# Delta rule: 32x32 inverses on GpSimd through HBM instead of five doubling levels on TensorE, and the last w_down halves by token tile

## The chip, the cores and the metric

The kernel runs on one core of a Trainium2 chip. A NeuronCore has a matrix engine (TensorE, PE), three elementwise engines (VectorE, DVE; ScalarE, ACT; GpSimd, POOL), a queue for transfers (SyncE, SP) and 16 DMA engines between HBM and the on-chip memory (SBUF). Matrix results land in PSUM, eight banks of 128 x 512 f32, which GpSimd can't read. Each engine executes its own list of instructions in order; they wait for one another by semaphores. Transfers are issued by SP and by ScalarE, each with a queue of its own.

The metric is the device time of one execution in microseconds (us), median of several.

## The reference

Two transformer blocks over 256 tokens of width 2048, all in float32. The first has a chunked mLSTM, a gated delta rule with a short convolution ahead of it, and output projections under gates; the second has windowed attention, gated linear attention in both directions and a SwiGLU network of width 5632; each block ends in an RMS norm. The part that the change touches is the solve of the delta rule, for 16 heads of width 128:

```
a_mat = where(strict, beta * (k k^T) * decay, 0)
lhs   = a_mat + eye
sol   = triangular_solve(lhs, rhs, lower, unit_diagonal)
u     = w_val - w_k S ;  o = q S + (q k^T * decay) u
```

and the end of the second block:

```
x = x + (silu(h @ w_gate) * (h @ w_up)) @ w_down
return rmsnorm(x, final_norm_w)
```

## The kernel before

**Products.** Nearly all arithmetic is in products of 256 tokens (two token tiles of 128) with weights from HBM. A job is a block of 512 output columns (JOBS; dk0, mq0, ..., d3 for w_down). It is cut into halves of 256 contraction rows; there are NH = 780 halves. Each weight is split into a high part (ScalarE, weight_hi) and a low part (VectorE, weight_lo), so that a float32 product becomes three fast ones: for each half, 2 row blocks x 2 token tiles x 3 = 12 matmuls of 512 columns, lines 1289 to 1291.

**Slots.** Everything else is a side step. side_table() gives each a slot, which is the number of the half that it stands ahead of: TensorE executes in slot s the side steps of s and then product(s). ScalarE and VectorE execute their parts of the side steps of s and then the split of half s + 3 (AHEAD). The weight ring holds four halves (RING), the raw ring three chunks of 1 MB (RAW), each of two halves. SP issues the load of chunk ci once both halves of chunk ci - 3 are split, which is at the splits of slot 2 ci - 8. Rows of activations for w_out and w_down are split by split_rows in rings of three (LRING).

**Delta rule.** Four groups g of four heads; slots run from s = END[dz g] + 1 = 35, 107, 163, 235. dk, dss, dkscale, dkc prepare k; drhs, ddecay, dmask the decays; dsc (s + 8 to s + 13) the scores, whose units (8 blocks of 128 x 128 for each group: four heads, two token tiles) are in the blocks B0 and PB. Then the inverse of the unit triangular blocks is built by doubling: dlev0 (s + 14) starts with the identity less the first level, dT transposes it, and for levels 1 to 6 dX (line 989), dY for U (line 999) and dY for T (line 1004, not in the last level) multiply 128 x 128 by 128 x 64 f32 blocks, with a copy by ScalarE, a subtraction by VectorE, and masks (LVL) and memsets by GpSimd between them. dv, du0, dbu, du1, do use the inverse; donorm, dgate and dout (s + 38) finish.

**Memory.** block_table() and bank_table() list the lives of the blocks of 4 KB a partition in the arena, and of the four side banks of PSUM, in step order; settle() places them, and a user of a block or bank waits for the last reader of what was there.

**End.** After d3's last product, res4(3) adds both tiles to the residual, sqsum takes the squares, nscale (with GpSimd's power -1/2) the scale, final scales four blocks of 512 columns, and SP stores them as four transfers of 512 KB.

**Start.** cols0 transposes the first norm columns when they have landed; xturn("u1", m) transposes two blocks of x and writes their high and low parts, at slot m - 2.

Of the kernel before, what the change touches and what calls it, by code (L numbers as in the profile page):

```python
# [62 lines left out]
LEVELS = 7  # L63
# [4 lines left out]
def host_constants():  # L68
# [5 lines left out]
    levels = []  # L74
    for l in range(LEVELS):
        w = 2 << l
        levels.append((r // w == c // w) & (r % w < w // 2) & (c % w >= w // 2))
    first = base + levels + [np.where(c > r, NEG, 0.0)]
# [13 lines left out]
    return {"const_first": np.concatenate([np.asarray(m, f) for m in first], axis=1),  # L92
            "const_second": np.concatenate([np.asarray(m, f) for m in second], axis=1),
# [125 lines left out]
def side_table():  # L219
# [26 lines left out]
    for g in range(4):  # L246
# [13 lines left out]
        for q in range(6):  # L260
            put(s + 8 + q, "dsc", g, q)
# [5 lines left out]
        put(s + 30, "du0", g), put(s + 31, "dbu", g), put(s + 32, "du1", g)  # L267
        put(s + 33, "do", g, 0), put(s + 34, "do", g, 1)
        put(s + 35, "donorm", g), put(s + 36, "dgate", g)
        put(s + 38, "dout", g, 0), put(s + 38, "dout", g, 1)  # L270
# [79 lines left out]
    for n in range(4):  # L350
        s = END[f"d{n}"]
        put(s, "res4", n), put(s, "sqsum", "r4", n)
        if n < 3:
            put(s + 1, "fweight", n)
    put(NH, "nscale", "r4")
    for n in range(4):
        put(NH, "final", n)
# [3 lines left out]
def gla_at(put, hp, s, v, t):  # L361
# [4 lines left out]
    for hh in range(2):  # L366
        for z in range(3):
# [16 lines left out]
    "delta": ("dk", "dss", "dkscale", "dkc", "drhs", "ddecay", "dmask", "dsc", "dlev0", "dT", "dX", "dY", "dv", "du0",  # L384
# [6 lines left out]
    "ffn": ("res2", "fact", "fturn", "res4", "fweight", "final"),  # L391
# [5 lines left out]
    "pe": {"ddecay": ("rest", "a", "b", "c"), "dY": ("", "T"), "ggate1": ("", "r")},  # L397
    "act": {"gate1": ("tanh", "exp", ""), "ddecay": ("a", ""), "gsum": ("q", "k", "")},
    "dve": {"cols0": ("",), "nscale": ("mean", ""), "gate1": ("v", "z", "arg", "u", ""), "dss": ("", "ck"),
            "dY": ("T", "U"), "donorm": ("mean", ""), "mscore": ("w", "den"), "msq": ("mean", ""),  # L400
            "ggate1": ("v", ""), "gsum": ("end", "rest", ""), "gsq": ("mean", ""), "alog": ("b", "")},
    "pool": {"dlev0": ("first", "", "zero")},
}
for _engine, _names in {
# [3 lines left out]
               "ggate2 gkend gsq gout alog aturn aout fturn final",  # L408
        "dve": "cols xturn kept silu gate0 gate2 fsum rel0 rel1 convtap convsilu dkscale ddecay dsc dlev0 dv dbu do "
               "dgate mdec mm mden mgate mgated yb ya yres x1w ggate0 ggate2 gscore gstate ggated apv res2 res4 fact "  # L410
               "fturn fweight final",
        "pool": "nscale dss drhs dmask dX dY donorm dgate mrhs msq ya gsq"}.items():
# [4 lines left out]
def signals(engine, name, args, part):  # L417

    if name == "dX" and engine == "pool":
        return args[1] < LEVELS - 1  # L420
    if name == "dY" and engine == "pool":
        return args[1] + 2 < LEVELS
    if name == "dY" and part == "T":
        return args[1] < LEVELS - 1
# [4 lines left out]
    if name == "final" and engine == "act":  # L429
        return args[0] < 3  # L430
# [15 lines left out]
def block_table():  # L446
# [31 lines left out]
    for g in range(4):  # L478
# [8 lines left out]
        live(("U", g), ("dlev0", g), ("pe:du1", g))  # L487
# [45 lines left out]
def bank_table():  # L533
# [6 lines left out]
    for step in STEPS:  # L540
# [12 lines left out]
        elif name == "dY":  # L553
            t.append((step + ("U",), step, (("dve:dY:U",) + args,), None))
            if args[1] < LEVELS - 1:
                t.append((step + ("T",), step, (("dve:dY:T",) + args,), None))
# [61 lines left out]
def _build(nc, ctx, a, out):  # L618
# [238 lines left out]
    def tensor_program(e):  # L857
# [441 lines left out]
        for slot in range(-AHEAD, NH + 2):  # L1299
# [3 lines left out]
            if 0 <= slot < NH:  # L1303
                product(slot)
# [1055 lines left out]
```

## Time and profile before

| | |
|---|---|
| time, median of 3 runs | 2563.59 us (2562.94 to 2566.3) |
| profiled execution | 2556.28 us |
| its span | 2554.1 us |
| TensorE busy | 2512.2 us, 98% |
| VectorE / ScalarE / GpSimd busy | 57% / 47% / 8% |
| whole weight loads | 387 of 1 MB, 5.1 us each from issue to landing |

The profile page gives busy time by engine, the span in slices, the chain that ended last and groups of instructions. Matmuls are pipelined: two of them overlap in the records, so the spacing of their starts says what one costs, not its duration. An f32 matmul of the side steps is recorded as two instructions, a transpose as one. A wait shows as idle time before an instruction, with what released it.

### The profile page before, as it was taken

To read this page: it belongs to the slowest core of one execution; us is meant where nothing else is said; L and a number is where in the kernel's file an instruction comes from. 1 tells how busy PE (TensorE), PEld (TensorE's weight loads), DVE (VectorE), ACT (ScalarE), POOL (GpSimd) and SP (SyncE) were. 2 spreads that over 40 slices of the span, in tenths; PEclk is the share of its full clock that TensorE was granted. 3 is DMA by queue.
4 is the path that set the end of the run, shared out by engine and by line. 5 is a ranking of instruction groups with operands and counts; after the bars stand their busy time and mean duration, and the time that the engine had idled before them with its cause. 6 is when DMAs were issued, how large, how long until landed. Compare 5 with 4: busy or idle time off the path is not lost.

```text
span 2554.1 us, 29749 instructions
## 1 busy us (share of the span) xinstructions
PE 2512.2 (98%) x12194; PEld 2073.3 (81%) x12194; DVE 1455.3 (57%) x1732; ACT 1196.7 (47%) x1662; POOL 202.7 (8%) x147
## 2 busy tenths in 40 slices
PE   8999999999999999999989999999999999999998
PEld 7888888888888888888877778767788888888886
DVE  6654665475456644556664544546555555456675
ACT  6533453354245434555654444546444444445654
POOL 0032003202310130000000000000000000000000
PEclk9999999999999999999999999999999999999999
DMA  6543454254345434666546444335655655555553
GB/s 221 180 149 100 150 187 148 92 169 160 116 132 165 165 116 133 211 208 208 200 157 209 149 148 144 122 114 191 206 190 189 191 188 190 189 190 189 181 196 134
DMA packets 220968, 426.52 MB, mean 167 GB/s; under 512 B 13766, under 2 KB 16079, under 8 KB 220834
## 3 DMA queue, kind: packets, MB, share of 16 engines
q1 hardware_dynamic: 213248, 411.72, 49.0%
q10 hardware_dynamic: 7586, 12.92, 1.5%
q8 instruction: 96, 1.57, 0.2%
q14 instruction: 38, 0.31, 0.0%
HBM read 420.39 MB, written 4.23 MB: 166 GB/s over the span
## 4 chain that ended last, share of the span: by engine, by line
PE 67%; issue 29%; DVE 2%; DMA 1%; ACT 1%; POOL 0%; SPq 0%; ACTq 0%; POOLq 0%; DVEq 0%
PE gemm L1289 18%; PE gemm L1291 18%; PE gemm L1290 18%; PE side L862 3%; PE side L999 2%; PE side L989 2%; PE side L1004 1%; DMA arena<-x 1%; PE side L1211 1%; PE side L1246 1%; DVE arena L1686 1%; PE side L1225 1%; PE side L964 1%; DVE weight_lo L1680 0%; DMA arena<-in_x_dram 0%
## 5 line engine op out<-in xcount | busy, mean ns | idle before, releaser
L1680 DVE TENSOR_TENSOR weight_lo<-weight_raw,weight_hi 128x1024 fp32r<-128x1024 f32 x780 | 975.4, 1253 | 792.4 <-ACT weight_hi L1311 790.9
L1311 ACT ACTIVATE weight_hi<-weight_raw 128x1024 fp32r<-128x1024 f32 x780 | 821.3, 1055 | 785.9 <-PE gemm L1291 764.2
L1289 PE MATMUL gemm<-weight_hi,x_hi 128*128 128x512 f32 x2368 | 954.7, 403 | 0.0
L1291 PE MATMUL gemm<-weight_hi,x_lo 128*128 128x512 f32 x2368 | 927.0, 391 | 0.0
L1290 PE MATMUL gemm<-weight_lo,x_hi 128*128 128x512 f32 x2368 | 924.2, 390 | 0.0
L1289 PEld LDWEIGHTS gemm<-weight_hi,x_hi 128*128 128x128 f32 x2368 | 446.4, 189 | 96.4 <-issue 11.3
L1291 PEld LDWEIGHTS gemm<-weight_hi,x_lo 128*128 128x128 f32 x2368 | 445.5, 188 | 97.2
L1290 PEld LDWEIGHTS gemm<-weight_lo,x_hi 128*128 128x128 f32 x2368 | 446.8, 189 | 89.1 <-issue 2.4
L1289 PE MATMUL gemm<-weight_hi,lhs_hi 128*128 128x512 f32 x736 | 289.5, 393 | 5.7 <-DVE lhs_lo L1680 5.6
L1291 PE MATMUL gemm<-weight_hi,lhs_lo 128*128 128x512 f32 x736 | 287.2, 390 | 0.0
L1290 PE MATMUL gemm<-weight_lo,lhs_hi 128*128 128x512 f32 x736 | 287.0, 390 | 0.0
L1311 ACT ACTIVATE arena<-side 128x512 f32<-128x512 f32 x109 | 64.3, 598 | 277.7 <-PE side L989 151.5
L1289 PEld LDWEIGHTS gemm<-weight_hi,lhs_hi 128*128 128x128 f32 x736 | 138.6, 188 | 37.2 <-DVE weight_lo L1680 8.0
L2207 POOL TENSOR_TENSOR stats<-stats,minus_half 128x4 f32<-128x4 f32 (+3 forms) x19 | 27.7, 1457 | 1731.2 <-DVE stats L1683 1731.2
L1291 PEld LDWEIGHTS gemm<-weight_hi,lhs_lo 128*128 128x128 f32 x736 | 138.5, 188 | 29.3
L1290 PEld LDWEIGHTS gemm<-weight_lo,lhs_hi 128*128 128x128 f32 x736 | 138.7, 188 | 28.1
L1680 DVE TENSOR_TENSOR lhs_lo<-arena,lhs_hi 128x512 fp32r<-128x512 f32 x184 | 128.2, 697 | 0.5 <-ACT lhs_hi L1311 0.5
L862 PE MATMUL side<-constants,arena 128*128 128x128 f32 (+4 forms) x668 | 99.0, 276 | 23.6 <-DMA constants<-in_const_first_dram 7.4
L862 PEld LDWEIGHTS side<-constants,arena 128*128 128x128 f32 (+4 forms) x668 | 81.0, 141 | 44.2 <-issue 8.5
L1311 ACT ACTIVATE lhs_hi<-arena 128x512 fp32r<-128x512 f32 x184 | 113.3, 616 | 1.1 <-PE gemm L1291 1.1
L2207 POOL TENSOR_TENSOR arena<-arena,phase_constants 128x512 f32<-128x512 f32 x56 | 78.5, 1422 | 142.9 <-PE side L989 78.7
L1680 DVE TENSOR_TENSOR arena<-arena,side 128x512 f32<-128x512 f32 x48 | 31.2, 685 | 67.5 <-PE side L1004 57.9
(184 smaller groups left out, 1354.5 us busy)
## 6 DMA issues: line engine op xcount, KB each, us to landing
weight_raw<-in_w_in_dram SPq DMA_DIRECT2D x207, 1024.0 KB, 5.1
weight_raw<-in_w_out_dram SPq DMA_DIRECT2D x48, 1024.0 KB, 5.1
weight_raw<-in_w_gate_dram SPq DMA_DIRECT2D x44, 1024.0 KB, 5.2
weight_raw<-in_w_up_dram SPq DMA_DIRECT2D x44, 1024.0 KB, 5.2
weight_raw<-in_w_down_dram SPq DMA_DIRECT2D x44, 1024.0 KB, 5.1
arena<-rel_line ACTq DMA_DIRECT2D x8, 384.0 KB, 4.9
arena<-in_x_dram SPq DMA_DIRECT2D x4, 512.0 KB, 9.4
arena<-in_final_norm_w_dram ACTq DMA_DIRECT2D x4, 512.0 KB, 7.1
```

Source lines behind the costliest of these rows:

```text
L862: return e.transpose(o, i, IDN[0:n, 0:n])
L964: m = e.matmul(p[:, (h % 2) * T:(h % 2 + 1) * T], yk[:, h * T:h * T + P], y[:, h * T:(h + 1) * T], start=True, stop=True)
L989: m = e.matmul(packed(p, n, wd), BM[:, n], sided(Tt[:, n], wd, 0), start=True, stop=True)
L999: m = e.matmul(packed(p, n, wd), X[:, n], sided(U[:, n], wd, 1), start=True, stop=True)
L1004: m = e.matmul(packed(p, n, wd), U[:, n], sided(X[:, n], wd, 0), start=True, stop=True)
L1211: m = e.matmul(o, l, r, start=z == 0, stop=z == len(terms) - 1)
L1289: e.matmul(pair[i][:, :], xh[:, s], wh, start=first, stop=False)
L1290: e.matmul(pair[i][:, :], xh[:, s], wl, start=False, stop=False)
L1291: m = e.matmul(pair[i][:, :], xl[:, s], wh, start=False, stop=last)
L1311: return e.activation(o, i, ACT.Copy, scale=scale)
L1680: return e.tensor_tensor(o, x, y, op)
L2207: return e.tensor_tensor(o, x, y, op)
```

## The change

1. The levels of width 2 to 32 leave TensorE. nout(g) (SP's queue, s + 11) writes the 32 x 32 diagonal blocks of the units to HBM with eight transfers; nin(g) (ScalarE's queue, s + 13) reads them back so that a partition holds one whole block (32 blocks, each four times, for eight columns of the inverse each); dinv(g) (GpSimd, s + 13) solves them with 31 rounds of a multiply and a subtract; tout(g) (SP, s + 24) and tin(g) (ScalarE's queue, s + 26) bring the inverses back by way of HBM into the diagonal of Tt.
2. Levels 64 and 128 stay on TensorE: dT at s + 28, dX and dY at s + 29 to s + 32, on operands cut to the width. Units are read where they lie, without masks. The later steps stand four slots on (dv s + 33, dout s + 42). The order of the scores is 0, 1, 4, 2, 3, 5.
3. Start: seven matmuls on zeros ahead of cols0, xturn("u1", m) for m >= 2 one slot later.
4. End: for the last three halves (LRING), all products of token tile 0 stand ahead of those of tile 1, and a step tail(i) takes the place of res4(3), sqsum, nscale and final, tile by tile; eight stores of 256 KB.

```diff
-        put(s + 14, "dlev0", g)
-        put(s + 16, "dT", g, 0), put(s + 16, "dT", g, 1)
-        for l in range(1, LEVELS):
-            put(s + 15 + 2 * l, "dX", g, l), put(s + 16 + 2 * l, "dY", g, l)
-        put(s + 29, "dv", g, 0), put(s + 29, "dv", g, 1)
+        for z, q in enumerate((0, 1, 4, 2, 3, 5)):
+            put(s + 8 + z, "dsc", g, q)
+        put(s + 11, "nout", g), put(s + 13, "nin", g), put(s + 13, "dinv", g)
+        put(s + 24, "tout", g), put(s + 26, "tin", g)
+        put(s + 28, "dT", g, 0), put(s + 28, "dT", g, 1)
+        for z, wd in enumerate(LEVELS):
+            put(s + 29 + 2 * z, "dX", g, wd), put(s + 30 + 2 * z, "dY", g, wd)
+        put(s + 33, "dv", g, 0), put(s + 33, "dv", g, 1)
...
-        put(m - 2, "xturn", "u1", m)
+        put(m - 2 if m < 2 else m - 1, "xturn", "u1", m)
...
+        def nout(g):
+            e.dma_start(claim("S", g)[:, 0:SUB * SUB // 4], a["const_unit"][:, :]).then_inc(sem("dma:unit"), 16)
+            w.wait_ge(*at("dve:dsc", g, 4))
+            to = n_dram[g].rearrange("(i h b) r c -> i b r h c", i=2, h=HB)
+            B0, B1 = by_head(blk("B0", g)), heads(blk("PB", g), 0)
+            for b in range(NSUB):
+                s = slice(b * SUB, (b + 1) * SUB)
+                e.dma_start(to[0, b], B0[s, :, s]).then_inc(sem("dma:nout"), 16)
+                e.dma_start(to[1, b], B1[s, :, s]).then_inc(sem("dma:nout"), 16)
+        def tout(g):
+            w.wait_ge(*at("pool:dinv", g))
+            to = t_dram[g].rearrange("n (c q) r -> q n c r", q=4)
+            S = blk("S", g)[:, 2 * SUB * SUB // 4:3 * SUB * SUB // 4].rearrange("p (c r) -> p c r", r=SUB)
+            for q in range(4):
+                e.dma_start(to[q], S[q * SUB:(q + 1) * SUB]).then_inc(sem("dma:tout"), 16)
...
         for ci in range(CHUNKS):
+            while ci >= RAW and slot < 2 * (ci - RAW) - 1:
+                for name, *args in SIDE[slot]:
+                    if name in steps:
+                        steps[name](*args)
+                slot += 1
...
         def cols0():
+            w.wait_ge(sem("dve:zeros"), 1)
+            for i in range(7):
+                e.matmul(sides[3][:, :], xfer[:, 0:P], xfer[:, 0:NC], start=True, stop=True)
...
+        def dX(g, wd):
+            Tt, hw = units(blk("Tt", g)), wd // 2
+            if wd < P:
+                w.wait_ge(*at("act:dT", g, 1))
+                p = open_bank("dX", g, wd)
+                for n in range(2 * HB):
+                    for t in range(0, P, wd):
+                        s = slice(t, t + wd)
+                        m = e.matmul(p[s, n * hw:(n + 1) * hw], unit_of(g, n)[s, s], Tt[s, n, t:t + hw],
+                                     start=True, stop=True)
+            else:
+                w.wait_ge(*at("dve:dY", g, hw))
+                p = open_bank("dX", g, wd)
+                for n in range(2 * HB):
+                    m = e.matmul(p[hw:wd, n * hw:(n + 1) * hw], unit_of(g, n)[:, hw:wd], Tt[:, n, 0:hw],
+                                 start=True, stop=True)
             m.then_inc(sem("pe:dX"))
...
+            if slot == NH - LRING:
+                for idx in range(slot, NH):
+                    product(idx, (0,))
             if 0 <= slot < NH:
-                product(slot)
+                product(slot, (0, 1) if slot < NH - LRING else (1,))
...
+        def nin(g):
+            w.wait_ge(*at("dma:nout", g))
+            src = bass.AP(tensor=n_dram.tensor, offset=g * 2 * HB * NSUB * SUB * SUB,
+                          ap=[[0, 4], [SUB * SUB, P // 4], [1, SUB * SUB]])
+            e.dma_start(claim("N", g), src).then_inc(sem("dma:nin"), 16)
+        def tin(g):
+            w.wait_ge(*at("dma:tout", g))
+            w.wait_ge(*at("pool:dinv:zero", g))
+            src = t_dram[g].rearrange("(n b) c r -> b c n r", b=NSUB)
+            Tt = units(blk("Tt", g))
+            for b in range(NSUB):
+                s = slice(b * SUB, (b + 1) * SUB)
+                e.dma_start(Tt[s, :, s], src[b]).then_inc(sem("dma:tin"), 16)
...
+        def tail(i):
+            b, (r, hr), total = blk("x2", 3), scale_of("r4"), stat(NT, "total", "r4")
+            if i == 0:
+                w.wait_ge(*at("pe:xturn", "u3", 7))
+                w.wait_ge(*at("act:sqsum", "r2", 3))
+                w.wait_ge(sem("pe:first_tile"), 1)
+            else:
+                w.wait_ge(*out_of("d3"))
+            tt(part(b, i), part(b, i), pair_of("d3")[i][:, :], ALU.add).then_inc(sem("dve:tail"))
...
+        def dinv(g):
+            e.memset(claim("X", g), 0.0)
+            e.memset(claim("Tt", g), 0.0).then_inc(sem("pool:dinv:zero"))
+            N = blk("N", g).rearrange("p (r c) -> p r c", c=SUB)
+            U, tmp, V = (blk("S", g)[:, z * SUB * SUB // 4:(z + 1) * SUB * SUB // 4] for z in range(3))
+            U = U.rearrange("p (r c) -> p r c", r=SUB)
+            w.wait_ge(*at("dma:nin", g))
+            w.wait_ge(*at("dma:unit", g))
+            for j in range(SUB - 1, 0, -1):
+                n = SUB // 4 - j // 4
+                c = slice(j // 4, SUB // 4)
+                by = tmp[:, 0:j * n].rearrange("p (r c) -> p r c", c=n)
+                after(tt(by, over(N[:, 0:j, j], 2, n), over(U[:, j, c], 1, j), ALU.mult))
+                after(tt(U[:, 0:j, c], U[:, 0:j, c], by, ALU.subtract))
+            e.tensor_copy(V.rearrange("p (c r) -> p r c", r=SUB), U).then_inc(sem("pool:dinv"))
```

## Rows read from the trace of the kernel before

**Rows 1.** The page, busy time (share of the span) and instructions by engine.

```profile
PE 2512.2 (98%) x12194; PEld 2073.3 (81%) x12194; DVE 1455.3 (57%) x1732; ACT 1196.7 (47%) x1662; POOL 202.7 (8%) x147
```

**Rows 2.** Timeline, ScalarE's first and last of five splits: start, us, instruction [idle before].

```profile
1399.08 1.06 ACT L1311 ACTIVATE weight_hi<-weight_raw 128x1024 fp32r<-128x1024 f32 x1 [1.36 <-PE gemm L1291]
...
1409.96 1.06 ACT L1311 ACTIVATE weight_hi<-weight_raw 128x1024 fp32r<-128x1024 f32 x1 [1.72 <-PE gemm L1291]
```

**Rows 3.** The chain that ended last, group 0's first level: start us, us, what.

```profile
175.93 1.73 PE side L989 x16
180.48 1.73 PE side L999 x16
182.22 1.79 PE side L1004 x16
186.82 1.73 PE side L989 x16
```

**Rows 4.** Groups by line and form: busy us, mean ns | idle before.

```profile
L989 PE MATMUL side<-arena 128*128 128x64 f32 x384 | 45.4, 271 | 0.0
```

**Rows 5.** Timeline of TensorE, gscore and the step behind it.

```profile
1438.02 1.15 PE L1168 MATMUL side<-arena 128*64 128x64 f32 x32
1439.10 0.66 PE L862 MATMUL side<-constants,arena 128*128 128x128 f32 x4
```

**Rows 6.** Timeline, group 0's scores: slots 45 and 48 on TensorE, VectorE's part.

```profile
152.19 1.02 PE L964 MATMUL side<-arena 128*128 128x256 f32 x4
...
163.09 1.05 PE L968 MATMUL side<-arena 128*128 128x128 f32 x8
...
153.33 0.69 DVE L1680 TENSOR_TENSOR arena<-side,arena 128x512 f32<-128x512 f32 x1 [1.88 <-PE side L964]
```

**Rows 7.** The stores' line: issue time on SP, ns min/median/max.

```profile
L852 SPq DMA_DIRECT2D out_dram<-arena x4: 384/497/1232, 2546.8 to 2548.6; - x4
```

**Rows 8.** DMA issues: count, KB each, median us from issue to landing.

```profile
weight_raw<-in_w_in_dram SPq DMA_DIRECT2D x207, 1024.0 KB, 5.1
...
x<-arena ACTq DMA_DIRECT2D x4, 512.0 KB, 6.0
...
rel_line<-arena ACTq DMA_DIRECT2D x1, 32.0 KB, 3.7
```

**Rows 9.** Groups of GpSimd by form: busy us, mean ns | idle before.

```profile
L2207 POOL TENSOR_TENSOR arena<-constants,gate_work 128x512 f32<-128x512 f32 x16 | 16.3, 1040 | 42.4 <-PE side L862 42.4
L2207 POOL TENSOR_TENSOR arena<-arena,stats 128x1024 f32<-128x1024 f32 x8 | 16.1, 2011 | 1.1 <-DVE stats L1680 1.1
...
L2207 POOL TENSOR_TENSOR stats<-stats,minus_half 128x4 f32<-128x4 f32 x6 | 6.0, 1007 | 459.8 <-DVE stats L1683 459.8
...
L2207 POOL TENSOR_TENSOR stats<-stats,minus_half 128x2 f32<-128x2 f32 x5 | 3.5, 699 | 880.6 <-DVE stats L1683 880.6
```

**Rows 10.** Timeline of the end, after TensorE's last matmul.

```profile
2541.76 1.29 DVE L1680 TENSOR_TENSOR arena<-arena,gemm 128x512 f32<-128x512 f32 x2 [6.87 <-PE gemm L1291]
2543.08 0.60 ACT L1363 ACTIVATE side<-arena 128x512 f32<-128x512 f32 x1 [8.91 <-DVE arena L1680]
...
2544.78 0.17 DVE L1683 TENSOR_SCALAR stats<-stats 128x2 f32<-128x2 f32 x1
2545.03 0.70 POOL L2207 TENSOR_TENSOR stats<-stats,minus_half 128x2 f32<-128x2 f32 x1 [723.14 <-DVE stats L1683]
...
2545.97 1.95 ACT L1311 ACTIVATE arena<-arena,stats 128x512 f32<-128x512 f32 x3 [1.41 <-DVE stats L1683]
```

**Rows 11.** Timeline of VectorE: two splits, beside GpSimd's products and after them.

```profile
144.13 2.77 DVE L1680 TENSOR_TENSOR weight_lo<-weight_raw,weight_hi 128x1024 fp32r<-128x1024 f32 x1 [0.66 <-ACT weight_hi L1311]
...
148.44 1.22 DVE L1680 TENSOR_TENSOR weight_lo<-weight_raw,weight_hi 128x1024 fp32r<-128x1024 f32 x1
```

**Rows 12.** Timeline of TensorE, matmuls of the first product.

```profile
12.51 0.63 PE L1289 MATMUL gemm<-weight_hi,x_hi 128*128 128x512 f32 x1
12.94 0.63 PE L1290 MATMUL gemm<-weight_lo,x_hi 128*128 128x512 f32 x1
```

More of the change, by code:

```diff
@@ L73, in host_constants @@
     base = [(r == c), (r > c), (r <= c), np.ones((P, P))]
[L74 to L78, printed above, removed]
+    first = base + [np.where(c > r, NEG, 0.0)]
+    column = (P // SUB) * np.arange(SUB // 4)[None, None, :] + (np.arange(P) // SUB)[:, None, None]
+    unit = np.arange(SUB)[None, :, None] == column
     same = r // GL_C == c // GL_C
@@ L349, in side_table @@
         put(s, "fact", n), put(s + 1, "fturn", n, 0), put(s + 2, "fturn", n, 2)
-    for n in range(4):
+    for n in range(3):
         s = END[f"d{n}"]
[L352 to L357, printed above, removed]
+        put(s, "res4", n), put(s + 1, "sqsum", "r4", n), put(s + 3, "fweight", n)
+    for i in range(NT):
+        put(NH, "tail", i)
     return side
@@ L670, in at @@
         if signal.startswith("dma:"):
-            return sem(signal), DMAS[signal]
+            return sem(signal), DMAS[signal] * (args[0] + 1 if args else 1)
         return sem(signal), ORDINAL[(signal,) + args]
-    DMAS = {"dma:rel0": 32, "dma:rel1": 16, "dma:ggate1": 64, "dma:const2": 16}
+    DMAS = {"dma:rel0": 32, "dma:rel1": 16, "dma:ggate1": 64, "dma:const2": 16,
+            "dma:nout": 128, "dma:nin": 16, "dma:unit": 16, "dma:tout": 64, "dma:tin": 64}
     def blk(*name):
@@ L982, in dX @@
-        def dX(g, l):
-            wd = 2 << l
-            BM, Tt = units(blk("BM", g)), units(blk("Tt", g))
-            w.wait_ge(*(at("pool:dlev0", g) if l == 1 else at("pool:dX", g, l - 1)))
-            w.wait_ge(*(at("act:dT", g, 1) if l == 1 else at("dve:dY:T", g, l - 1)))
-            p = open_bank("dX", g, l)
-            for n in range(2 * HB):
-                m = e.matmul(packed(p, n, wd), BM[:, n], sided(Tt[:, n], wd, 0), start=True, stop=True)
-            m.then_inc(sem("pe:dX"))
@@ L1259, in fturn, with product @@
             turn_pair(p, blk("z", f"fg{n}"), c).then_inc(sem("pe:fturn"))
-        def product(idx):
+        def product(idx, tiles=tuple(range(NT))):
             j, c, h = HALVES[idx]
@@ L1286, in product @@
                     continue
-                for i in range(NT):
+                for i in tiles:
                     s = slice(i * P, (i + 1) * P)
@@ L2300, in ya, with tail @@
             tt(b, b, blk("z", f"ga{n}"), ALU.add).then_inc(sem("pool:ya"))
+        def tail(i):
+            w.wait_ge(*at("dve:tail:mean", i))
+            power(scale_of("r4")[0][:, i:i + 1], stat(NT, "total", "r4")[:, i:i + 1]).then_inc(sem("pool:tail"))
         def gsq(hp):
@@ L2304, in gsq @@
             power(stat(2 * NT, "grr", hp), stat(2 * NT, "gssq", hp)).then_inc(sem("pool:gsq"))
[L2306 to L2307 removed]
+        steps = dict(nscale=nscale, dss=dss, drhs=drhs, dmask=dmask, dinv=dinv, donorm=donorm,
+                     dgate=dgate, mrhs=mrhs, msq=msq, ya=ya, gsq=gsq, tail=tail)
         for name, *args in STEPS:
```

254 lines of the change are left out of this document (122 added, 132 removed).

## The prediction, made before the change was run

> **What bounds the kernel now.** I read the page's busy shares first: TensorE's matmuls are busy 98% of the span, no other compute engine over 57% [rows 1]. The slots prove that this is a real bound and not only a long queue: where TensorE has nothing but weight products, one half of a chunk (12 matmuls) takes (1409.96 - 1399.08) / 4 = 2.72 us, slot after slot [rows 2]. ScalarE starts one weight split in each of them, and its start is set by the product that frees a ring place. So the end is the sum of TensorE's products and of the side steps put between them, and the question for each edit is how much of TensorE's own stream it takes away, and whether TensorE then waits for something that it did not wait for before. The chain of waits in order of time gives the side steps of the delta rule: 16 instructions each (8 matmuls in two passes) of the lines of dX, dY for U and dY for T [rows 3].
>
> **The inverses on TensorE.** From one dX to the next dX is 186.82 - 175.93 = 10.89 us [rows 3]. Two products are 2 x 2.72 = 5.44, so one level costs 5.45. Six levels less the T half of the last (1.79) [rows 3] are 6 x 5.45 - 1.79 = 30.9 us for a group of four heads, and four groups 124 us, all on the path. The count agrees: 384 dX instructions are 4 groups x 6 levels x 16 [rows 4].
>
> What stays: dT (eight transposes) is moved, not changed. New per group are dX for 64 with 16 matmuls (32 instructions), dY for 64 with 32 (64), dX for 128 and dY for 128 with 8 each (16 and 16): 128 instructions for 272. They are smaller: stationary operands of 64 or 32 columns, and for width 64 two tiles in turn at partitions 0 and 64. The nearest row is gscore, 128x64 stationary with its outputs in turn in the two halves of the partitions: 32 instructions between 1438.02 and 1439.10, 0.034 us each [rows 5]; the old form takes 1.73 / 16 = 0.108 [rows 3]. I take 0.034 for the 96 of width 64 (3.3 us) and, for the 32 of width 128, which stay in one half, the middle, 0.057 (1.8 us), and 0.1 for each of four changes from product to side step (a level shows 5.45 for 5.25 of side steps in two of them): 5.5 us. Saving 30.9 - 5.5 = 25.4 a group, **101.6 us** in all. Bounds: all at 0.108 leaves 30.9 - 14.2 = 16.7 (67 us in all); all at 0.034 gives 26.2 (105 us).
>
> The Trainium skill, "TensorE: Matmul & The Clock Gate", section on what happens when you issue a matmul, says that a weight load takes its number of columns over 1.2 GHz, so 107 ns for 128 columns and 53 for 64. The 0.108 of the old form agrees; gscore's 0.034 is below 53, so there loads of the two halves overlap. By the page alone the 128 new instructions would cost at most about 6.8 us where I take 5.1: 7 us more in all.
>
> **The new way round: where a wait may come back.** Take group 0 (s = 35); in the three others s, too, is odd, and between s+14 and s+28 there are only evictions and, in groups 1 and 3, one mnum, so the pattern repeats. Slots 43 to 48 carry the scores: slot 45's start at 152.19 and slot 48's at 163.09, 3.63 apart [rows 6]. Score 4 now comes at slot 45; VectorE's step there ends at 153.33 + 0.69 = 154.0 [rows 6]. dT is at slot 63: slot 49 starts at 166.7, and 14 bare slots of 2.72 later is 204.8. Between the two, **50.8 us**, lie in a row:
> - nout: eight DMAs on SP's queue. An issue takes about 0.5 us there (384/497/1232 ns) [rows 7], and the smallest stores to and from HBM land after 3.7 us [rows 8]: 4.0 + 3.7, lands at 161.7. ScalarE, whose nin is at slot 48, reaches it near 161 and waits little.
> - nin: 512 KB on ScalarE's queue, 6.0 us like the x stores [rows 8]: 167.7.
> - dinv on GpSimd: 31 rounds of a multiply and a subtract, each waiting for the one before. The elements are j x (8 - j // 4) summed over j = 31 to 1, 1560, twice 3120. From 128x512 (1040 ns) and 128x1024 (2011 ns) an element costs 1.90 ns and an instruction 0.07 us; from the powers of 2 and 4 columns (699 and 1007 ns) the fixed part is 0.39 us [rows 9]. A hand-over adds 0.08 (2544.78 + 0.17 to 2545.03) [rows 10]. So 62 x (0.15 to 0.47) + 5.9 + 0.5 for the copy = 16 to 36 us; I take 26, the middle, as neither row has short three-dimensional operands.
> - tout: four DMAs on SP, 2.0 + 3.7 = 5.7. SP reaches it only after the weight load at slot 58, near 194.
> - tin: four DMAs on ScalarE's queue, 5.7; ScalarE reaches its slot 61 near 198.
>
> 167.7 + 26 = 193.7, tout lands at 199.7, tin at 205.4: **0.6 us after TensorE comes for dT**. tout further stands behind a 1 MB weight load (5.1 us to land [rows 8]) issued just before it on the same queue, which can add up to about 3 us. I take 1.5 us of stall a group, 6 in all; bounds 0 and 12 us a group.
>
> The skill speaks against this edit: "DMA: Bandwidth & Descriptors", Specifications, wants at least 512 B a run and says that shorter ones are read, modified and written. nout, tout and tin move runs of 128 B. No row of before has a thousand such runs in one transfer. By it the three transfers would be nearer the long end, which is the rival "late" below.
>
> What waits behind the waits: behind nout and tout SP holds the weight loads. The load next after tout is due near 199 and is needed by ScalarE at slot 65, about 210; a load takes 5.1 us, so some 6 us of delay are covered. Behind nin and tin ScalarE holds its weight splits, which run three slots (8.2 us) ahead of their products: covered up to about 5 us. Behind tin's semaphore TensorE holds everything; that is the stall counted. GpSimd has no other step between s+13 and s+25 in any group; its next, msq at s+26 in two of them, comes after. VectorE is slowed while GpSimd multiplies: one weight_lo took 2.77 us at 144.13, and 1.22 at 148.44, when GpSimd was through [rows 11]. In these slots VectorE has one split (at worst 2.8 us in a slot of 2.72) and little else, and runs three slots ahead: nothing added. The level masks, memsets and the packed subtractions that go were hidden behind products: 0. The steps four slots on end in dout(3) at slot 277; the products that read it begin at slot 290: 0. The load of the phase constants, 64 KB instead of 512, comes after the start and beside products: 0.
>
> **Start.** The first products run with 0.43 us between matmuls (12.51 to 12.94) [rows 12] where 2.72 / 12 = 0.227 is usual; the clock view grants 1.00 there all the same, but the spacing is that of the lower level, 1.2 GHz. About eight matmuls do: 1.6 us. The seven zero matmuls (14 instructions of 512 columns, 0.43 each at 2.4 GHz and twice that at 1.2) fill TensorE from about 1.4 us to 9 to 13 us, while the first transposes could start at 7.4. So the clock's 1.6 us is won or as much lost; xturn one slot later lets the first product go before x's second part lands, about 0.3. Sum: **-0.5**, from -1.5 to +2.5.
>
> **Tail.** The last product ends just before VectorE's residual at 2541.76 [rows 10], near 2541.65; the span is 2554.1, so 12.4 us follow. Now the first token tile's tail lies under 18 matmuls (4.1 us) of the second. After the last: residual 0.65 (half of 1.29), square and its read 0.9, mean and power 0.35 + 0.8, two copies of 0.65 [rows 10], four issues on SP of 0.5 and a landing of the last near 3.5 instead of 2 MB of stores at once: 0.1 + 0.65 + 0.9 + 1.15 + 1.4 + 1.5 + 3.5 = 9.2. Gain **3.1**, from 2 to 4. The order of the three last halves adds no matmul, and their splits are ready: the last pair of rows needs the product before them, 2.7 us ahead of its use.
>
> **Sum.** Against the profiled execution, 2556.28 (span 2554.1): -101.6 + 6 - 0.5 - 3.1 = -99.2, 2457.1. The runs' median, 2563.59, is 7.3 above that execution, and I carry this over: **2464.4**.
>
> **Rivals.** *Late:* TensorE waits at dT(g, 0) because dinv is at its long end (36 us) or the 128 B runs land late. Each us past the 50.8 us costs four. With 5 to 12 us a group: 2479 to 2506, middle about 2488. For: the chain fits with no margin, and nothing in before measures its small pieces. Against: mine are not the cheapest values. *No shorter matmuls:* small tiles cost 0.108 each, as if the weight load of a full tile set the pace: 8.7 us more a group, 2499. Gscore's row speaks against. *Slower than before:* GpSimd's small instructions cost like the powers of 2 to 4 columns in full, 0.7 to 1.0 us, plus 0.08. It decides from dinv = 26 + 25 = 51 us on, 0.73 us an instruction and hand-over; at 0.93 us dinv is 58, the stall 33 a group, 132 in all, SP holds the weight loads meanwhile, and the time is about 2563.6 - 105 + 132 = 2590. Its power function speaks against, since the time grows with 154 ns an element, so that it is no price of a product. *Without effect:* stalls and savings cancel, 2563.
>
> **How the numbers follow.** Forecast 0.58 (2450 to 2478: all matmuls at 0.034 and no stall to 3 us of stall more a group); late 0.28; no shorter matmuls 0.07; slower 0.05; without effect 0.02. The range 2450 to 2495 holds the forecast and some two thirds of late. What a measurement of this kernel can tell from no change is about 0.2%, 5 us: faster 0.93, same 0.02, slower 0.05.
>
> **What would show it.** Right: TensorE's idle before dT's transposes at most 3 us; the side steps between slots 63 and 67 of a group sum to some 5.5 us; GpSimd's 62 instructions span 26 us; no wait of ScalarE's weight_hi on a weight load in these stretches; the end 9 us after the last matmul. Wrong: dT waits for the DMA of Tt, with its place in GpSimd (dinv ends after 194) or in the queues (dinv ends before, tin lands after 205); small matmuls spaced by 0.1 us; or a product waiting on weight_lo after tout.

## The result, and the profile after

The changed kernel takes **2508.87 us** (median of four runs, 2505.57 to 2511.7) against 2563.27 for the kernel before, run beside it: ratio 0.9783, 95% interval 0.977 to 0.9795. It is 2.2% faster, but 44.5 us slower than forecast and 14 us above the range. The profiled execution took 2509.5, its span 2507.8. The case that came true is the rival *late*: TensorE waits for dT in every group. With what hangs on the wait it costs 10.8 us a group, inside the 5 to 12 of that rival; the time is 3 us beyond its 2506 because other terms fell short too.

The page of the profiled execution after: busy time by engine, then the chain that ended last by engine (beside [rows 1]).

```profile
PE 2435.0 (97%) x11632; PEld 1983.1 (79%) x11632; DVE 1418.9 (57%) x1705; ACT 1191.0 (47%) x1647; POOL 229.2 (9%) x328
...
PE 85%; POOL 5%; DMA 3%; DVE 2%; issue 1%; ACT 1%; ACTq 0%; SPq 0%; POOLq 0%; DVEq 0%
```

TensorE's busy time fell by 77.2 us, the span by only 46.3. GpSimd, idle 91% of the time, now holds 5% of the chain: an engine that does little is on the path. The view of waits shows where (TensorE's waits: us in total, times, longest):

```profile
PE side L889 <- DMA arena<-delta_inverses: 32.8, 4, 8.9
PE side L889 <- DVE arena L1755: 13.0, 8, 3.6
```

L889 is the transpose helper, here in dT; it waits 8.2 us a group on average for the inverses from HBM. The chain of waits from the scores of group 0 to that dT (start us, us, what; only the pieces used below):

```profile
161.06 11.21 DMA arena<-delta_blocks
172.67 1.33 POOL arena L2281
...
186.00 1.22 POOL arena L2281
187.29 0.32 POOL arena L2281
...
204.85 0.67 POOL arena L2337
205.54 0.67 SPq L852
...
207.55 1.97 DMA delta_inverses<-arena
209.54 0.33 ACTq L1532
...
210.90 3.71 DMA arena<-delta_inverses
214.66 1.97 PE side L889 x8
```

And what TensorE does around it, in the timeline (start us, us, instruction [idle before]) and, below, in windows of 5 us (busy us and count by engine, then PEclk, DMA share, GB/s):

```profile
205.84 0.39 PE L1335 MATMUL gemm<-weight_hi,x_lo 128*128 128x512 f32 x1
214.66 1.97 PE L889 MATMUL side<-constants,arena 128*128 128x128 f32 x8 [8.43 <-DMA arena<-delta_inverses]
...
218.55 0.63 PE L1335 MATMUL gemm<-weight_hi,x_lo 128*128 128x512 f32 x1
218.98 0.63 PE L1333 MATMUL gemm<-weight_hi,x_hi 128*128 128x512 f32 x1
```

```profile
205.00:210.00 5.00, 1.22 (x6) 0.68 (x4) 0.00 (x0) 0.00 (x0) 0.52 (x1) 1.00 0.27 39
210.00:215.00 5.00, 0.34 (x2) 0.35 (x3) 2.36 (x2) 2.00 (x2) 0.00 (x0) 0.51 0.71 224
215.00:220.00 5.00, 5.00 (x17) 4.23 (x16) 1.23 (x1) 2.14 (x3) 0.00 (x0) 0.50 0.64 210
220.00:225.00 5.00, 5.00 (x52) 4.04 (x51) 0.52 (x1) 1.93 (x3) 0.00 (x0) 0.97 0.01 3
```

In the wait the granted clock drops to 0.50, the 1.2 GHz level, and stays there until about 220: dT takes 1.97 us where the same kind of eight takes 1.03 at 2.4 GHz, and some nine matmuls are 0.43 apart, not 0.23. That is 0.9 + 9 x 0.2 = 2.7 us more, so this wait of 8.4 us costs 11. The groups differ: behind the 8.9 us of group 2 only three matmuls are slow, behind the waits of groups 1 and 3 ten and eleven. In all, TensorE's busy time is 10.4 us above that of experiment 4, which has the same instructions and no wait at dT (2435.0 and 2424.6): 2.6 us a group on average.

### The profile page after: what moved, and what is told of

It is laid out like the page before. It is cut to its first block, busy times and chain, and to the rows that moved or that the text cites. A ratio compares the mean times of both kernels' runs of the same rounds, so it can differ in the third digit from the quotient of the medians.

```text
span 2507.8 us, 28796 instructions
## 1 busy us (share of the span) xinstructions
PE 2435.0 (97%) x11632; PEld 1983.1 (79%) x11632; DVE 1418.9 (57%) x1705; ACT 1191.0 (47%) x1647; POOL 229.2 (9%) x328
## 4 chain that ended last, share of the span: by engine, by line
PE 85%; POOL 5%; DMA 3%; DVE 2%; issue 1%; ACT 1%; ACTq 0%; SPq 0%; POOLq 0%; DVEq 0%
PE gemm L1333 25%; PE gemm L1335 25%; PE gemm L1334 25%; POOL arena L2281 5%; PE side L889 3%; DMA arena<-delta_blocks 2%; DMA arena<-x 1%; PE side L1254 1%; DVE arena L1755 1%; DVE weight_lo L1749 1%; PE side L1289 1%; PE side L1268 1%; PE side L994 0%; ACT weight_hi L1361 0%; PE side L899 0%
## 5 line engine op out<-in xcount | busy, mean ns | idle before, releaser
L1749 DVE TENSOR_TENSOR weight_lo<-weight_raw,weight_hi 128x1024 fp32r<-128x1024 f32 x780 | 960.0, 1233 | 799.2 <-ACT weight_hi L1361 797.7
L2281 POOL TENSOR_TENSOR stats<-stats,minus_half 128x4 f32<-128x4 f32 (+4 forms) x20 | 28.2, 1408 | 1757.6 <-DVE stats L1752 1757.6
L2281 POOL TENSOR_TENSOR arena<-arena 128x48 f32<-128x48 f32 (+21 forms) x256 | 133.0, 520 | 381.5 <-DVE arena L1755 300.6
L889 PE MATMUL side<-constants,arena 128*128 128x128 f32 (+4 forms) x668 | 104.7, 286 | 56.0 <-DMA arena<-delta_inverses 32.8
L889 PEld LDWEIGHTS side<-constants,arena 128*128 128x128 f32 (+4 forms) x668 | 83.0, 146 | 80.6 <-DMA arena<-delta_inverses 34.5
L1361 ACT ACTIVATE arena<-side 128x512 f32<-128x512 f32 (+2 forms) x93 | 54.6, 588 | 167.4 <-PE side L889 92.8
L1430 ACT ACTIVATE arena<-gemm,stats 128x512 f32<-128x512 f32 x66 | 41.8, 685 | 46.6 <-PE gemm L1335 46.6
```

Source lines behind the costliest of these rows:

```text
L889: return e.transpose(o, i, IDN[0:n, 0:n])
L1361: return e.activation(o, i, ACT.Copy, scale=scale)
L1430: s = e.activation(part(b, i), pair_of(key)[i][:, :], ACT.Tanh, scale=hr[:, i:i + 1])
L1749: return e.tensor_tensor(o, x, y, op)
L2281: return e.tensor_tensor(o, x, y, op)
```

## The experiments

Each ratio is to the kernel before, run again beside the experiment; its interval is 0.3 to 0.5% wide, 8 to 12 us. The first four go at the cause from four sides: the number of the rounds, their length, their layout, and the time allowed.

**1. Only one round of elimination.**

```diff
-            for j in range(SUB - 1, 0, -1):
+            for j in range(1, 0, -1):
```

> The changed kernel with 1 of the 31 rounds of elimination on GpSimd left in each group (two instructions instead of 62, so the inverses are wrong); all transfers stay. Theory A, the chain through GpSimd (its 33 us of rounds) is simply too long for the four slots: the wait for dT falls from 8.0 to 9.3 us a group to nothing, the half clock after it goes too (2.6 us a group), and the time is 2461 to 2467. Theory B, the transfers are what is late (short runs of 128 bytes behind the weights on the queues): the wait falls by less than half, 2485 to 2500. Theory C, the loss is not in the wait but in GpSimd working beside VectorE: below 2460, and clearly below what moving the readers later (run e4_later4) gives.

Measured: 2466.19 us, ratio 0.9627 [0.9607, 0.9647]. 1.0 us of the wait for the inverses is left in all. Theory A: the transfers alone, 128-byte runs and all, would have been in time.

**2. Ten products more a group.**

```diff
                 after(tt(U[:, 0:j, c], U[:, 0:j, c], by, ALU.subtract))
+                if j % 3 == 0:
+                    after(tt(by, over(N[:, 0:j, j], 2, n), over(U[:, j, c], 1, j), ALU.mult))
```

> The changed kernel with ten of the products on GpSimd done twice in each group (72 instructions instead of 62, nothing else changed): by the durations of these shapes in the profile (0.24 to 0.48 us, with 0.08 between two) that is 4.6 us a group. Theory A: each us lands in the wait for dT in full, +18 to +20 us, 2527 to 2529; theory B: part of it hides beside the transfers, under +10.

Measured: 2524.16 us, ratio 0.9854 [0.9831, 0.9877]: 15 us over the changed kernel by the medians, 18 by the ratios. The forecast of the experiment, +18 to +20, is missed by a little: the 72 instructions span 36.22, 37.60, 36.22 and 37.23 us, 3.6 to 4.1 more than the 62 and not 4.6, 15.4 in all. Of these 13.6 are in the wait for dT, which rose from 32.8 to 46.4 us. So what the rounds take longer, TensorE waits longer, nearly in full.

**3. U kept by columns**, fewer and longer rows in each instruction (the constant, tout's source and the copy change with it).

```diff
-                by = tmp[:, 0:j * n].rearrange("p (r c) -> p r c", c=n)
-                after(tt(by, over(N[:, 0:j, j], 2, n), over(U[:, j, c], 1, j), ALU.mult))
-                after(tt(U[:, 0:j, c], U[:, 0:j, c], by, ALU.subtract))
+                by = tmp[:, 0:j * n].rearrange("p (c r) -> p c r", c=n)
+                after(tt(by, over(N[:, 0:j, j], 1, n), over(U[:, c, j], 2, j), ALU.mult))
+                m = tt(U[:, c, 0:j], U[:, c, 0:j], by, ALU.subtract)
...
```

> The same inverses with U kept by columns on GpSimd, so that the patterns of an instruction have 1 to 8 rows of up to 31 elements instead of up to 31 rows of 1 to 8 elements, and the copy at the end goes (0.66 us). If an instruction's price follows its rows (0.19 us, 8.7 ns a row and 0.85 ns an element, fitted to the shapes of the changed kernel's trace) the 62 take 26 us instead of 32.5, the wait falls to about 2 us a group, and the time by 27 to 37 us: 2472 to 2482. If it follows elements, only the copy is saved: -3, 2506.

Measured: 2512.98 us, ratio 0.9809 [0.9794, 0.9824]. Both expectations missed. The 62 instructions took 33.12 us where they had taken 32.45; the price by rows, which I had fitted to the mean durations of the shapes, doesn't show. Those means mixed two kinds of the same shape. Taken one by one, GpSimd's and VectorE's instructions read like this in the changed kernel (timeline, one stretch of group 0):

```profile
180.03 0.27 POOL L2281 TENSOR_TENSOR arena<-arena 128x48 f32<-128x48 f32 x1
180.37 1.21 POOL L2281 TENSOR_TENSOR arena<-arena 128x48 f32<-128x48 f32 x1
181.66 0.30 POOL L2281 TENSOR_TENSOR arena<-arena 128x69 f32<-128x69 f32 x1
...
180.21 1.23 DVE L1749 TENSOR_TENSOR weight_lo<-weight_raw,weight_hi 128x1024 fp32r<-128x1024 f32 x1 [1.50 <-ACT weight_hi L1361]
```

The first two have one shape; one takes 0.27 us, the other, which began while VectorE's weight_lo ran, 1.21, and ends 0.14 after weight_lo does (180.21 + 1.23 = 181.44). In group 0, 11 of the 62 are like this and take 13.1 us together; the other 51 take 14.5, 0.28 each. With U by columns other instructions meet the split (the two of 31 elements take 0.26 and 0.25, the first of 30 takes 1.23), again 11 of them, and the sum stays. Experiment 5 tests whether the split is the cause.

**4. Four slots more for the chain.**

```diff
-        put(s + 24, "tout", g), put(s + 26, "tin", g)
-        put(s + 28, "dT", g, 0), put(s + 28, "dT", g, 1)
+        put(s + 26, "tout", g), put(s + 28, "tin", g)
+        put(s + 32, "dT", g, 0), put(s + 32, "dT", g, 1)
...
```

(and each step from dX to dout four slots later).

> The changed kernel with the inverses as they are, their readers (dT and all steps behind it) another four slots later and the transfers out and in two slots later: TensorE has 17 us more work before it comes for dT. Theory A: the wait of 8 to 9 us and the half clock behind it go: 2461 to 2468. Theory B (what is late is the queue of transfers, which starts later too): some 5 us a group stay, 2480 to 2490. Theory C (GpSimd's work beside the others costs): over e1_norounds by 5 us or more. Rival of its own: steps four slots later collide with those of the mLSTM and the next group, 2475 to 2490 with waits on VectorE.

Measured: 2466.01 us, ratio 0.9629 [0.9614, 0.9645], the time of experiment 1, with the inverses made in full. Theory A; C falls, since GpSimd's rounds beside the others cost nothing that these runs can tell. (The 17 us in the expectation are wrong: the steps behind dT move with it, and four bare slots are 4 x 2.72 = 10.9 us. That still covers 8 to 9.) The transfers moved too, and not all is hidden: in group 0 a product waits 2.33 us, because ScalarE's splits stand behind tin, which waits for the inverses to reach HBM.

```profile
218.12 0.50 PE L1333 MATMUL gemm<-weight_hi,x_hi 128*128 128x512 f32 x1 [2.33 <-DVE weight_lo L1749]
```

**5. VectorE's splits cut to an eighth beside the inverses**, so that the low parts of the weights there are stale.

```diff
+            first = (idx % 2) * n
+            if any(END[f"dz{g}"] + 1 + 16 <= idx <= END[f"dz{g}"] + 1 + 34 for g in range(4)):
+                n = n // 8
-            tt(wlo[:, idx % RING, 0:n], raw[:, idx // 2 % RAW, (idx % 2) * n:(idx % 2 + 1) * n],
+            tt(wlo[:, idx % RING, 0:n], raw[:, idx // 2 % RAW, first:first + n],
```

> The changed kernel, with VectorE's subtraction that makes weight_lo done on one eighth of its elements (128 of 1024 columns) in 19 halves of each group, from 12 slots before dT to seven behind it; the rest of those low parts is stale, so the products there are off. In the trace of the changed kernel 12 of GpSimd's 62 instructions take 1.1 to 1.3 us instead of 0.3, and each ends when a weight_lo that began beside it ends. Theory D, the two engines shut each other out while both read two operands of SBUF: the long ones vanish, the 62 take about 62 x (0.29 + 0.08) = 23 us instead of 33, no wait for dT is left: 2463 to 2468. Rival: the length comes from a transfer or from GpSimd itself, 33 us and 2509 stay.

Measured: 2468.37 us, ratio 0.9621 [0.9602, 0.9641]. The inverses of group 0 in the timeline of this kernel, and in that of the changed one:

```profile
172.38 22.94 POOL L2284 TENSOR_TENSOR arena<-arena 128x31 f32<-128x31 f32 x62 [21.89 <-DMA arena<-delta_blocks]
```

```profile
172.34 32.45 POOL L2281 TENSOR_TENSOR arena<-arena 128x31 f32<-128x31 f32 x62 [21.50 <-DMA arena<-delta_blocks]
```

Nothing of GpSimd's work was changed, and it fell by 9.5 us; no instruction is over 1 us any more. So theory D: a GpSimd instruction that starts while VectorE subtracts two SBUF operands isn't through until that has ended.

The trace of the changed kernel has the contrast that the run lacks. Of the 248 instructions of the four groups 46 are long, and each ends 0.11 to 0.21 us after a VectorE instruction that began before it and reads two operands in SBUF: 44 times weight_lo, twice another. The six VectorE instructions there with an operand in PSUM (gemm) lengthen none. Group 1, VectorE and then GpSimd:

```profile
447.28 1.28 DVE L1755 SCALAR_TENSOR_TENSOR arena<-arena,gemm 128x512 f32<-128x512 f32 x2
...
449.75 1.32 DVE L1755 SCALAR_TENSOR_TENSOR arena<-arena 128x1024 f32<-128x1024 f32 x1
```

```profile
448.02 0.32 POOL L2281 TENSOR_TENSOR arena<-arena 128x66 f32<-128x66 f32 x1
...
450.06 1.16 POOL L2281 TENSOR_TENSOR arena<-arena 128x60 f32<-128x60 f32 x1
```

The Trainium skill, "SBUF — State Buffer", section "Who interferes with whom", says just this: a VectorE instruction with two SBUF inputs and a GpSimd instruction that reads SBUF hold a read port in turn, whole instructions long, whichever starts first. Both directions are in this case: [rows 11] show the other, 2.77 us for a weight_lo beside GpSimd.

**6. dT one slot later, transfers in place.**

```diff
-        put(s + 28, "dT", g, 0), put(s + 28, "dT", g, 1)
+        put(s + 29, "dT", g, 0), put(s + 29, "dT", g, 1)
...
```

> The changed kernel with dT and all steps behind it one slot later, transfers where they are. One bare slot is 2.72 us of TensorE's work, so the wait falls from 8.5 to 5.8 us a group. If TensorE's clock still falls to 1.2 GHz in the shorter wait: -11 us, 2498. If it doesn't: -21 us, 2488.

Measured: 2509.02 us, ratio 0.9784 [0.9765, 0.9803]; nothing was gained. In groups 0 and 2 the wait for dT fell as expected, to 6.1 and 6.3 us. In groups 1 and 3 it went over to another step. Timelines of group 1: TensorE at mout, ScalarE, and GpSimd's msq.

```profile
468.69 1.11 PE L889 MATMUL side<-constants,arena 128*128 128x128 f32 x4 [9.74 <-DVE arena L1755]
...
460.45 1.82 ACTq L1532 DMA_DIRECT2D arena<-delta_inverses  x4
462.31 0.47 ACT L1576 ACTIVATE arena<-side,stats 128x256 f32<-128x256 f32 x1 [13.06 <-issue]
...
464.53 1.01 POOL L2281 TENSOR_TENSOR stats<-stats,minus_half 128x4 f32<-128x4 f32 x1 [8.00 <-DVE stats L1752]
```

msq's squares (L1576) are at the slot of tin, s+26, and stand behind tin on ScalarE, which waits for the inverses to reach HBM. mgated needs msq, and mout, at s+28, needs mgated. So an mLSTM step waits for the delta rule through ScalarE's queue.

**7. nin as four DMAs.**

```diff
-                          ap=[[0, 4], [SUB * SUB, P // 4], [1, SUB * SUB]])
-            e.dma_start(claim("N", g), src).then_inc(sem("dma:nin"), 16)
+                          ap=[[SUB * SUB, P // 4], [1, SUB * SUB]])
+            for q in range(4):
+                e.dma_start(N[q * SUB:(q + 1) * SUB], src).then_inc(sem("dma:nin"), 16)
...
```

> The changed kernel with nin (512 KB into 128 partitions, one DMA whose outermost dimension has four entries) as four DMAs of 32 partitions each. The single one took 11.2 us from its issue, and in most of it the DMA engines were busy to 0.26, as if 4 of 16 worked. Theory E: the split brings it over all 16, it lands 4 to 6 us earlier, less three more issues of 0.5 us on ScalarE's queue; the wait for dT falls by 3 to 5 us a group: 2489 to 2497, lower if the half clock behind the wait shrinks too. Rival: the weight load issued 0.9 us earlier holds it up; it lands when it did, 2509.

Measured: 2494.88 us, ratio 0.9726 [0.9704, 0.9747]. In the chain of waits of this kernel, from nin's last issue to the first round:

```profile
161.78 0.47 ACTq L1525
162.28 5.38 DMA arena<-delta_blocks
168.06 0.28 POOL arena L2283
```

5.4 us from the last issue and 6.8 from the first, instead of 11.2, and GpSimd starts at 167.72 instead of 172.34. The wait for dT is 19.6 us in all, for 32.8. In the packets of the two traces nin moves from 164.4 to 171.3 in the changed kernel and from 164.0 to 167.0 here. So the bytes, their runs and the weight load before them are the same, and the rival of the experiment is out; what changed is the outermost dimension, 32 for 4, and the number of DMAs. One DMA with its dimensions in another order was not run. The changed kernel between the weight loads (windows of 1 us, DMA share next to last):

```profile
166.00:167.00 1.00, 1.00 (x6) 0.84 (x5) 1.00 (x2) 0.00 (x0) 0.00 (x0) 1.00 0.25 98
167.00:168.00 1.00, 1.00 (x7) 0.81 (x6) 0.27 (x1) 0.00 (x0) 0.00 (x0) 1.00 0.26 106
```

The Trainium skill, "DMA: Bandwidth & Descriptors", "Rules for kernel authors", has the rule: a DMA whose outermost dimension is a broadcast of c copies runs on at most c of the 16 engines. The share of 0.25 to 0.26 in the changed kernel agrees with 4 of 16.

**8. Experiment 4 with the old start.**

```diff
-        put(m - 2 if m < 2 else m - 1, "xturn", "u1", m)
+        put(m - 2, "xturn", "u1", m)
...
-            for i in range(7):
-                e.matmul(sides[3][:, :], xfer[:, 0:P], xfer[:, 0:NC], start=True, stop=True)
...
```

> The kernel of e4_later4 (readers of the inverses four more slots on) with the start of the kernel before: no seven matmuls on zeros, xturn in its old slots. The changed kernel's slot 43 began 1.27 us later than before's, although its first products run at the full clock. If that is the price of the new start: 1.3 us under e4_later4, 2464.7. If the forecast's sum held (-0.5 for the new start) and the 1.27 us come from elsewhere: 0.5 over it. The difference is near what the runs can tell; the trace at slot 43 decides.

Measured: 2463.53 us, ratio 0.961 [0.9587, 0.9633]. The intervals of 4 and 8 overlap, so the runs don't settle it; the traces do. Slot 43's scores begin at 145.00 here, at 146.20 in experiment 4 and in the changed kernel, at 144.93 before: the new start costs 1.2 us. Of the versions run, this has the lowest time.

**9. Experiment 4 with tout and tin in their old slots.**

```diff
-        put(s + 26, "tout", g), put(s + 28, "tin", g)
+        put(s + 24, "tout", g), put(s + 26, "tin", g)
```

> The kernel of e4_later4 with the transfers out and in back in their old slots (tout two slots earlier, tin two slots earlier), dT and the rest four slots later as there. In e6_later1 the wait left dT in the second group and came up whole (9.74 us) at mout, one step ahead: its msq stands on ScalarE's queue behind tin's wait for the inverses. Theory F, tin's place decides as much as dT's: in the second and fourth group TensorE waits 9 to 11 us at mout, with some half clock behind it: 2486 to 2494. Rival: only dT's distance counts: 2466.

Measured: 2496.67 us, ratio 0.9737 [0.9721, 0.9754]: 28 us over experiment 4 by the ratios, 31 by the medians, for two transfers *issued from earlier slots*. TensorE's timeline in groups 0 and 1:

```profile
214.00 0.80 PE L1333 MATMUL gemm<-weight_hi,x_hi 128*128 128x512 f32 x1 [4.88 <-DVE weight_lo L1749]
```

```profile
465.51 1.12 PE L889 MATMUL side<-constants,arena 128*128 128x128 f32 x4 [11.27 <-DVE arena L1755]
```

Theory F, with more than it said: mout waits 11.3 us in group 1, and in group 0 a *product* waits, since ScalarE's weight splits stood behind tin too ([12.73 <-issue] before the first of three) and used up their lead. The time is 3 us above the experiment's range, which counted no wait in groups 0 and 2.

**10. Two slots later, transfers with them.**

```diff
-        put(s + 28, "dT", g, 0), put(s + 28, "dT", g, 1)
+        put(s + 30, "dT", g, 0), put(s + 30, "dT", g, 1)
...
```

> The changed kernel with readers and transfers two slots later instead of four: 5.4 us more for the chain. Theory A and F: no wait at mout, since tin now comes after msq; 8.0 to 9.3 less 5.4 leaves 3 us at dT, 12 us in all, and 0 to 10 us of half clock behind it: 2478 to 2488. If a wait of 3 us leaves the clock at 2.4 GHz, the low end.

Measured: 2477.97 us, ratio 0.9664 [0.9648, 0.9681], at the low end of what was expected, though the clock did fall. The waits of TensorE for the inverses are two, together 8.9 us, in groups 0 and 2:

```profile
PE side L889 <- DMA arena<-delta_inverses: 8.9, 2, 5.0
```

In group 0, where TensorE waits 5.03 us, the granted clock averages 0.83 between 215 and 225, and the twelve transposes from dT on take 2.5 us until the next product starts, for 1.2 in experiment 4. In group 1 dT doesn't wait at all, and mout 1.55 us.

## Why the prediction was wrong, step by step

**What held.** The bound (TensorE's own stream) and the price of the small matmuls. Without the wait the kernel comes to 2463.5 to 2468.4 (experiments 1, 4, 5, 8). The forecast of 2464.4 has 6 us of stall in it; without them it is 2458.4, so 5 to 10 us are missing here too (see below, errors that cancel). The small matmuls of group 0, by the timeline after:

```profile
221.09 1.12 PE L1020 MATMUL side<-arena 64*64 64x32 f32 x32
...
225.48 0.69 PE L1038 MATMUL side<-arena 64*32 64x32 f32 x32
226.10 1.12 PE L1042 MATMUL side<-arena 64*64 64x32 f32 x32
...
230.51 1.15 PE L1026 MATMUL side<-arena 128*64 128x64 f32 x16
```

From start to start of what follows these are 1.05 + 0.62 + 1.06 for the 96 of width 64 (2.73 us, forecast 3.3), and 1.07 for each 16 of width 128 (0.067 an instruction, forecast 0.057 as "the middle" of 0.034 and 0.108, which is 0.071; 1.08 for the fourth line, dY): 4.9 us for 5.1. The rival *no shorter matmuls* is out. Tail: the last matmul starts at 2498.34, so it ends near 2498.66 and 9.15 us follow, forecast 9.2. That fit is closer than its terms: two copies of 0.65 stand in the sum with 1.4, four issues of 0.5 with 1.5.

```profile
2498.34 0.39 PE L1335 MATMUL gemm<-weight_hi,lhs_lo 128*128 128x512 f32 x1
2498.61 5.80 SPq L879 DMA_DIRECT2D out_dram<-arena  x8
2500.67 0.56 POOL L2281 TENSOR_TENSOR stats<-stats,minus_half 128x1 f32<-128x1 f32 x1 [3.46 <-DVE stats L1752]
```

**What failed: the stall, 6 us in the sum, was 33, with 10 of half clock behind it.** The step that failed is the chain from the scores to dT, in two links: dinv beside VectorE's splits, and nin. Along the chain of group 0, where I had dT's input at 205.4 and it came at 214.6:

- *dinv*, "62 x (0.15 to 0.47) + 5.9 + 0.5 ... I take 26, the middle": measured 32.45 + 0.07 + 0.66 = 33.2. It is inside the bounds, but for another reason than the bounds have: the undisturbed instructions are under the middle (22.9 + 0.7 = 23.6 in experiment 5). The step that failed is the sentence on VectorE: I read in [rows 11] that a split is stretched to 2.77 us beside GpSimd, asked what that does to VectorE, and found "nothing added". The same row says that the two engines slow each other, and there is a split in every slot of 2.72 us. Eleven or twelve of them, 0.9 us each, are 10 us on the chain. The engine off the path was asked, not the one on it.
- *nin*, 6.0 "like the x stores": 11.2 from its issue (GpSimd starts at 172.3, not 167.7). The row was that of a transfer of the same bytes, not of the same shape.
- *tout and tin*, 11.7 together: 9.15. Runs of 128 bytes were no trouble: nout's 16 KB landed in 2.3 us, tout's 32 KB in 2.0, tin's in 3.9. The forecast had them too long. The Trainium skill's line on runs under 512 B ("DMA: Bandwidth & Descriptors", Specifications), weighed in the forecast against the edit, is about reaching the full rate; in these small transfers no cost of it shows.
- Sum: +4.6 + 7.2 - 2.6 = 9.2 us later than forecast, and 0.6 were forecast; TensorE itself came 1.4 later (206.2 for 204.8). 9.2 + 0.6 - 1.4 = 8.4, the wait. From there each us cost one, as forecast.

So the rival *late* came true by neither of the two reasons that it names: dinv is short of its 36 us, and the 128 B runs land earlier than forecast.

**What the sum left out.** The wait's after-effect, 2.6 us a group on average: there is no term for the clock after a stall, though the start had one. The cover of the queue behind tin ("three slots (8.2 us) ahead of their products: covered up to about 5 us") was right in kind; experiments 9 and 4 show its end. And the steps that now stand four slots on add small waits on VectorE (L1755, 13.0 us for 5.8 on the same helper before), about 7 us in all; in experiment 4, with the stall gone, 10.0 are left and 2.6 for weight_lo come in.

**Start**, -0.5 forecast, +1.2 to 1.3 measured. The first product now runs at full speed, as forecast, but it starts later. Before and, below, after:

```profile
11.09 0.78 PE L1289 MATMUL gemm<-weight_hi,x_hi 128*128 128x512 f32 x1
...
15.48 0.60 PE L862 MATMUL side<-constants,arena 128*128 128x128 f32 x4
```

```profile
1.45 8.17 PE L899 MATMUL side<-gate_work 128*128 128x512 f32 x14 [1.45 <-DVE gate_work L1767]
9.55 1.25 PE L889 MATMUL side<-constants,arena 16*128 16x16 f32 x9
12.37 0.47 PE L1333 MATMUL gemm<-weight_hi,x_hi 128*128 128x512 f32 x1 [1.56 <-DVE x_lo L1755]
...
15.18 0.60 PE L889 MATMUL side<-constants,arena 128*128 128x128 f32 x4
...
19.80 0.47 PE L1333 MATMUL gemm<-weight_hi,x_hi 128*128 128x512 f32 x1 [0.54 <-DVE x_lo L1755]
```

The zero matmuls end at 9.6, where the first transposes had begun at 7.37, and the first product starts 1.3 us later. The clock gives that back: it is through at 15.18, for 15.48 before. The loss comes behind it, where xturn stands a slot later: from the end of the second product to the start of the third are 1.14 us for 0.35, 0.54 of them a wait for x_lo, and ahead of the seventh 0.89 for 0.36. No run parts the zero matmuls from xturn's slots; this is read from the traces. The value is inside the term's range, the sign was wrong.

**Two errors that cancel.** Experiment 4's span is 2463.4, where the sum without its stall gives 2449 (2554.1 - 105.2): the term of 101.6 was too large by 12.9. Taken between GpSimd's power functions in dss, group 0 to 1 went from 384.75 - 122.29 = 262.5 us to 363.92 - 123.55 = 240.4: 22.1 saved for 25.4; the next two saved 23.8 and 24.2, and from there to the last matmul 18.6. Of the 14 us that are missing, the start is 1.8 (its forecast and its cost), and TensorE's waits behind the start are 4.9 (25.9 us for 21.0 before). The clock is some 4: in steps that both kernels have, mostly after 870 us, 19 more matmuls of the products are 0.43 apart in experiment 4's trace (mean granted clock 0.994, before 0.996). The last 4 are not traced. The forecast then added 7.3 us, the distance of the profiled run to the median, and that was no property of the kernel: after it is -0.6. On record the kernel before takes 2558.5 us at a granted clock of 0.996 and 2567.9 at 0.991, so its profiled run was one with a high clock. So the agreement at 2464 to 2466 is closer than the sum deserved.

**Chances.** *Late* had 0.28 and was the truth. (Its "middle about 2488" should have been 2492, at 8.5 us a group.) "The chain fits with no margin" was the reason to give it more: 0.6 us of excess on a chain of 51, with one term known to 20 us, is no base for a stall of 1.5.

## What to carry over

When work leaves the bottleneck for another engine, build its chain from issue to use, and price each link on the engine that is now on the path, with the neighbours that share its port: ask of every row that shows two engines slowing each other what it does in both directions. A chain that just fits doesn't fit; give it slack by moving its readers, since four slots of slack cost nothing here that the runs can tell, and a late us costs one and a fall of the clock. And a DMA that waits holds all that its queue's engine does: put it where its data is ready, not where it could first be asked for.

## What the runs showed of the hardware that was not expected

- GpSimd's three-dimensional products of 8 to 76 elements took 0.20 to 0.35 us each undisturbed, whichever way the pattern lay, and 1.0 to 1.3 us when they began beside a 1.23 us subtraction of VectorE; beside one of its instructions with an operand in PSUM they stayed at 0.32 to 0.34.
- A DMA of 512 KB whose outermost dimension had four entries took 11.2 us and kept the DMA engines 0.26 busy for part of it; four of 128 KB took 5.4 us after the last issue. The packets themselves took 6.9 and 3.0 us.
- After 8.4 us without matmuls TensorE's granted clock was 0.50 for some 5 us of full work. In the same trace three matmuls were at half speed after 8.9 us without and ten after 8.0, and in experiment 2, after 12.4 us, two, so a longer wait was not followed by a longer fall.
- Two matmul streams on 64-row tiles in alternation ran 0.019 (32 columns stationary) to 0.033 us an instruction.
